# A hybrid decoder trunk on one core: weights issued ahead of cached pages, and evictions taken between the operations of the rotation

## The reference

```python
h = rmsnorm(x, norm_g);  proj = h @ w_in        # 1024 -> all mixers and gates
out_lru = (rg_lru(conv(lru_x)) * silu(lru_z)) @ w_lru_out
q, k = rope(rmsnorm(nsa_q)), rope(rmsnorm(nsa_k))
o_nsa = g0 * o_cmp + g1 * o_slc + g2 * o_win    # block means, top 16 blocks of 64, window of 512
out_nsa = (o_nsa * silu(nsa_z)) @ w_nsa_out     # keys and values: new rows and, for samples, cached pages
out_dn = (rmsnorm(gated_delta(conv(dn_qkv))) * silu(dn_z)) @ w_dn_out
merged = sigmoid(m0) * out_lru + sigmoid(m1) * out_nsa + sigmoid(m2) * out_dn
x = x + merged @ w_out
```

## Time and profile before

| what | value |
|---|---|
| median of 3 runs (lowest to highest) | 2092.81 us (2089.54 to 2092.93) |
| profiled execution, its own time | 2090.35 us |
| its span, first to last instruction | 2088.5 us |
| mean granted TensorE clock | 0.945 |
| busy, share of the span: PE, DVE, ACT, POOL | 88%, 45%, 25%, 4% |
| DMA, mean over the span | 81 GB/s |

### The profile page before, as it was taken

One profiled execution on the slowest core, in us unless ns is written; L12 is line 12 of the kernel. 1 busy time (PEld: TensorE's weight loads), 2 busy tenths in 40 slices (PEclk: granted clock), 3 DMA queues, 4 the chain that ended last, 5 costly groups with the idle time before them and its releaser, 6 DMA issues.

```text
span 2088.5 us, 29550 instructions
## 1 busy us (share of the span) xinstructions
PE 1842.8 (88%) x11486; PEld 1323.4 (63%) x11486; DVE 946.0 (45%) x2208; ACT 515.9 (25%) x1161; POOL 91.5 (4%) x133
## 2 busy tenths in 40 slices
PE   7999999998499955599999999999984998655999
PEld 5777787875355644477467767888652556444763
DVE  2558546336265432243135675453462653333421
ACT  3143211123266310110112341111322662110100
POOL 0001000011000000000000010100120000000000
PEclk9999999989799987899999999999997999887999
DMA  6214111123410233426042141111333103443321
GB/s 214 67 60 106 42 42 42 56 72 85 129 51 11 82 110 101 133 89 187 1 162 64 61 106 42 26 37 56 109 92 104 31 11 93 123 118 97 113 88 46
DMA packets 196528, 170.07 MB, mean 81 GB/s; under 512 B 49248, under 2 KB 186898, under 8 KB 195942
## 3 DMA queue, kind: packets, MB, share of 16 engines
q1 hardware_dynamic: 192164, 150.11, 24.7%
q0 software_dynamic: 4064, 18.03, 2.7%
q10 hardware_dynamic: 162, 0.05, 0.0%
HBM read 153.67 MB, written 21.71 MB: 84 GB/s over the span
## 4 chain that ended last, share of the span: by engine, by line
PE 75%; DVE 10%; SPq 7%; issue 4%; DMA 3%; ACT 1%; ACTq 0%; DVEq 0%
PE PS L920 49%; PE PS L849 5%; SPq L643 3%; DVE arena L1854 3%; DMA ring<-in_w_in 3%; SPq L655 3%; PE PS L1292 2%; PE PS L1305 2%; PE PS L1140 1%; PE PS L1122 1%; DVE arena L1780 1%; PE PS L1142 1%; PE PS L1361 1%; PE PS L1211 1%; PE PS L1026 1%
## 5 line engine op out<-in xcount | busy, mean ns | idle before, releaser
L920 PE MATMUL PS<-hT,ring 128*128 128x288 f32 x2624 | 692.3, 411 | 6.4 <-DVE arena L2057 3.7
L920 PEld LDWEIGHTS PS<-hT,ring 128*128 128x128 f32 x2624 | 488.4, 191 | 143.9 <-issue 11.7
L920 PE MATMUL PS<-zs,owr 128*128 128x288 f32 x768 | 215.6, 424 | 126.2 <-DVE sg L1786 126.2
L920 PEld LDWEIGHTS PS<-zs,owr 128*128 128x128 f32 x768 | 143.5, 197 | 170.5 <-DVE sg L1786 127.6
L920 PE MATMUL PS<-tt,ws 128*128 128x288 f32 x672 | 190.4, 415 | 11.8 <-DVE sg L1910 4.4
L849 PE MATMUL PS<-con,arena 128*128 128x128 f32 (+5 forms) x934 | 148.5, 286 | 13.4 <-DMA arena<-in_nsa_k_norm 10.7
L849 PEld LDWEIGHTS PS<-con,arena 128*128 128x128 f32 (+5 forms) x934 | 111.6, 144 | 74.2 <-issue 46.0
L920 PEld LDWEIGHTS PS<-tt,ws 128*128 128x128 f32 x672 | 120.7, 190 | 51.9 <-DVE sg L1910 8.0
L1786 DVE TENSOR_TENSOR ws<-ring 128x512 f32<-128x512 f32 x84 | 58.1, 691 | 201.8 <-DMA ring<-in_w_in 200.3
L920 PE MATMUL PS<-arena 128*128 128x512 f32 (+1 forms) x320 | 124.8, 594 | 2.1 <-DVE sg L1910 2.1
L1783 DVE TENSOR_TENSOR sg<-PS,sg 128x288 f32<-128x288 f32 x132 | 60.3, 457 | 134.6 <-PE PS L920 132.6
(11 more groups left out here) (303 smaller groups left out, 2060.9 us busy)
## 6 DMA issues: line engine op xcount, KB each, us to landing
ring<-in_w_in SPq DMA_DIRECT2D x54, 1024.0 KB, 5.4
arena<-in_cache_nsa_kv SPq DMA_DIRECT2D x128, 192.0 KB, 2.5
ring<-in_w_in SPq DMA_DIRECT2D x32, 256.0 KB, 4.3
arena<-in_state_nsa_win SPq DMA_DIRECT2D x32, 256.0 KB, 3.3
arena<-in_cache_nsa_kv SPq DMA_DIRECT2D x128, 64.0 KB, 1.8
arena<-in_w_out SPq DMA_DIRECT2D x4, 2048.0 KB, 8.1
out_win_sample<-in_state_nsa_win POOLq DMA_DIRECT2D x2, 4032.0 KB, 23.1
arena<-in_x_prompt SPq DMA_DIRECT2D x8, 512.0 KB, 5.3
```

Source lines behind the costliest of these rows:

```text
L920: ins = mm(to, w, x, start=start, stop=stop, skip_group_check=True)
```

## The change

On SyncE, `weights` and `out_weights` of the attention and sample stages are moved ahead of page loads: tile 22 ahead of the three waits and of the first key pages; `out_weights` 4 and 5 and tile 23 between the first key and value pages; tile 24 and `out_weights` 6 to 9 follow the first value pages. In the loop over pairs, `weights(25+k2)` becomes the first call of a step (it was behind both page batches), and the two `out_weights` come between the key pages and the wait for `s_pv`. The same DMAs are issued, with the same waits of their own.

On DVE, `take_to` is called at three places in the rotation of the key rows: after the product of `zs`, between the first two multiplies, and ahead of the addition.

```diff
@@ SyncE @@
                 out_weights(l * NO + 3)
+                weights(l * NS + 22)
                 sp.wait_ge(s["b_out"], l * 32 + 32)
                 sp.wait_ge(s["dn_ok"], past["dn_ok"] + 1)
                 sp.wait_ge(s["qk_ok"], past["qk_ok"] + 2)
                 cached_keys(0)
                 window_keys(0)
+                out_weights(l * NO + 4)
+                out_weights(l * NO + 5)
+                weights(l * NS + 23)
                 cached_values(0)
                 window_values(0)
-                for g in (22, 23, 24):
-                    weights(l * NS + g)
-                    for o in range(2):
-                        out_weights(l * NO + 2 * (g - 20) + o)
+                out_weights(l * NO + 6)
+                out_weights(l * NO + 7)
+                weights(l * NS + 24)
+                out_weights(l * NO + 8)
+                out_weights(l * NO + 9)
                 sp.wait_ge(s["a_p"], past["a_p"] + N_UNIT)
                 window_keys(1)
                 window_values(1)
                 for k2 in range(DEC_BATCH // 2):
+                    weights(l * NS + 25 + k2)
                     if k2 < DEC_BATCH // 2 - 1:
                         sp.wait_ge(s["s_t"], past["s_t"] + 6 * (k2 + 1))
                         cached_keys(k2 + 1)
                         for b in (2 * k2 + 2, 2 * k2 + 3):
                             window_keys(b)
+                    for o in range(2):
+                        out_weights(l * NO + 10 + 2 * k2 + o)
+                    if k2 < DEC_BATCH // 2 - 1:
                         sp.wait_ge(s["s_pv"], past["s_pv"] + k2 + 1)
                         cached_values(k2 + 1)
                         for b in (2 * k2 + 2, 2 * k2 + 3):
                             window_values(b)
-                    weights(l * NS + 25 + k2)
-                    for o in range(2):
-                        out_weights(l * NO + 10 + 2 * k2 + o)
@@ VectorE @@
                 mul(zs[:, 8:12], zs[:, 8:12], dc[:, 0:4]).then_inc(s["dn_ok"], 1)
+                normed = began[("bc_ok", past["bc_ok"] + 10)]
+                take_to(normed + 1)
...
                     link(mul(y, y, rep(C("sin"), m - n)))
                     if n == 0:
                         take_before("kt_t", 2)
+                    else:
+                        take_to(normed + 2)
                     link(mul(x, x, rep(C("cos"), m - n)))
                     if n == 0:
                         take_before("kt_t", 3)
+                    else:
+                        take_to(normed + 3)
                     add(x, x, y).then_inc(s["qk_ok"], 1)
```

## The result

| what | before | after |
|---|---|---|
| median of 4 runs (lowest to highest), us | 2092.87 (2089.54 to 2095.19) | 1887.76 (1882.57 to 1889.64) |
| profiled execution, its own time, us | 2090.35 | 1882.57 |
| its span, us | 2088.5 | 1880.8 |
| mean granted TensorE clock | 0.945 | 0.995 |

The ratio is 0.9017, 95% interval 0.8995 to 0.9039: faster by 205 us. The forecast was 1887 for the median and 1884.4 for the profiled execution. In the code after, the lines of TensorE, of ScalarE and of VectorE's helpers stand 6 higher (L920 is L926, L1786 is L1792), VectorE's lines behind the rotation 12 (L2251 is L2263); those of SyncE's loads are unchanged.

The account below looks back on a forecast made before the run. Weight tiles queued behind page loads on SyncE were taken to stall VectorE and then TensorE. 139.4 + 62.6 - 3.0 + 7.0 = 206.0 us off 2090.35 gave 1884.4, a median of 1887; range 1876 to 1912.

Parts of the forecast that it names:

- Pair loop: Three later sample pairs of each layer: with the weight tile issued first, halts and slow restarts go, worth 139.4 us.
- slow restart: TensorE after each halt: it runs on at the lower clock, costing 2.2 us each time.
- rival 1: Pair loop: SyncE's queue becomes the bound, 38.75 us a step against TensorE's 36.75; 12 us, giving 1899; chance 0.12.
- bound kept for late keys: Pair loop: last keys taking the weights' 5.4 us make the third batch 1.3 us late, 2.6 both layers; taken as 0.
- rule that the prediction weighed: Pair loop: key pages behind a 1 MB tile on one ring report after it; sum 2.6 us smaller, taken as 0.
- Attention: Attention stage, both layers: tile 22 issued earlier removes the halt and restart, 62.6 us, less 3 for late `out_weights` 4.
- 1.5 us taken off for `out_weights` 4 coming late: Attention, each layer: `out_weights` 4, now behind the first keys, is next late; bounds nothing or 4 us, -3 in all.
- Rotation: Key-row rotation on VectorE: evictions taken between its operations let TensorE's transposes start earlier; 3.5 us a layer, 7.0.
- Rival 2: Attention: the halt only moves, to `out_weights` 4 or tile 23; 59.6 us back, giving 1947; chance 0.05.
- Rivals 3 and 4: SyncE: 3, the tile leaves when it did, 2086 or 2093, chance 0.01; 4, pages late instead, 2132, chance 0.02.

## Why the prediction was right

**The size.** Profile to profile 207.7 us came, 3.4 of them in unchanged code; 204.3 is the change's, and the terms had 206.0.

**Pair loop, predicted 139.4, measured 136.6.** The reading that a tile is late by what stands before it on SyncE's queue held, and so did the slow restart after each halt: without halts the granted clock stays 1.00. Missing are 0.72 + 0.85 + 0.95 = 2.5 us of new waits, all in the last pair of a layer. That is rival 1 in small, and it comes from a step that was mis-sized: the margin was worked out with a step of 38.75 us, and the trace has 39.27 for the first and 40.07 for the second (750.13 to the next tile at 790.20). The row of one `weights` was taken at its 0.51 us, but SyncE's next page load begins 0.77 us later (710.86 + 0.51 to 712.14), and likewise 0.78 behind the output weights (730.03 + 1.06 to 731.87), which in turn took 1.06 us and not 1.6. The run with the windows on GpSimd, its step 1.6 us shorter, has none of these waits. The bound kept for late keys, 1.3 us a layer, was of the right size; late `owr` in this loop was in no term, though the prediction's own times have no margin for it: the last pair's two `out_weights` are issued from 805.8 to 807.4 and take 4.6 us or more, and TensorE wants them 2.5 us into the pair (774.64 - 0.72 - 771.38), at 811.2.

**The ring order.** Key pages directly behind the tile took 2.5 to 5.6 us to land (shortest and longest of 712 to 731), and 2.3 to 3.2 in the batch of 670 to 690, which isn't directly behind one; their medians are 3.2 and 2.4. In 712.14 to 729.01 the DMA engines were busy 0.81, where before it was 0.59. This agrees with the rule that the prediction weighed (the Trainium skill, "DMA: Bandwidth & Descriptors", Queues, rings and completion order): what stands behind a large transfer on a ring reports later. But it is the batch's first pages that pay (5.4 to 5.6 us for the first two, 2.6 to 3.0 for the last three), and TensorE waits for the last. The one late batch, 0.95 us in layer 1, isn't the ring's doing either: its last three pages landed in 2.4 to 3.0 us, and the wait is gone when SyncE's step is shorter while pages still follow the tile. So taking 0 for the rule was right. The tile itself took longer than assumed, 7.4 to 9.7 us in the pair loops against the 5.4 of the earlier trace rows; the 10 us that it was early covered it.

**Attention, predicted 59.6, measured 59.6, and that close by luck.** Three errors of one layer met. The first: the 1.5 us taken off for `out_weights` 4 coming late weren't lost. It went out at 530.20 and TensorE used it at 536.42 without a wait; its two DMAs landed in 4.1 to 4.3 us. From issue to use are 6.2 us, and 6.2 and 6.1 in the two runs with the old rotation, so the rotation's gain, which moves keys and use alike, isn't the reason. The prediction had 3.9 us there (538.6 to 542.5). It let `out_weights` 4 leave when the value pages used to, and counted its use as if the whole halt went.

That is the second error: the last 1.9 us of the halt stay. They are the work that the tile releases on VectorE, three weight sums, and behind them the reduction and ScalarE's eviction on which TensorE's next score waits. VectorE before and after, where the sums begin:

```profile
561.95 0.69 DVE L1786 TENSOR_TENSOR ws<-ring 128x512 f32<-128x512 f32 x1 [26.98 <-DMA ring<-in_w_in]
```

```profile
527.37 0.68 DVE L1792 TENSOR_TENSOR ws<-ring 128x512 f32<-128x512 f32 x1
```

Before, TensorE went on at 566.02, 4.07 us after the sums began; after, at 531.42, 4.05 us after. TensorE's own steps now cover 2.16 of it, and 1.89 stay open. VectorE has no pause from the sums to that reduction at 529.29; no run took the sums away. The third: the restart was worth 2.7 us and not 2.2. Between the first score and the first pooling of layer 0 TensorE was busy 135.45 us before and 132.76 after, with the same 711 passes. In sum 1.5 + 0.5 - 1.9 = 0.1 us a layer.

**Rotation, predicted 7.0, measured 4.1 + 4.1 in the trace,** 6.5 with its interval 4.0 to 8.8 from the takes alone. The gaps of 2.4 + 1.0 were 2.07 + 0.63, and the query rows begin 3.5 us earlier, once the 3.4 ahead are taken off, for the predicted 3.0. TensorE's first transposes come 4.1 earlier; the prediction worked out 3.7 and took 3.5.

**The rivals.** Rival 1 came with 2.5 us of its 12. Rival 2 (the halt only moves) didn't come in the whole change, but the run with the tile alone shows it for the pair loop: it is what happens when one of the two transfers is left behind the pages. I had costed the two as one edit; that they are worth 137 us together, and apart 41 and nothing that can be told, stood nowhere in the prediction. Rivals 3 and 4 are excluded by SyncE's timeline: the tile leaves at 710.86 and the key pages follow it at 712.14.

## What to carry to other kernels

A transfer is late by what stands before it on its in-order queue, waits included: compare the time at which it is issued with the time at which its slot came free, and move together *all* transfers that the same user needs, since one left behind keeps most of the stall. Before moving, lay the queue's whole step, gaps between different kinds of issue included, beside the consumer's period: here the new order has next to nothing to spare by the last pair, and 9 us more per batch cost a third of the gain. Not all of a halt goes with its cause: the work that the late transfer releases is in it too, so follow that chain on each engine, not only on the queue, and keep what TensorE has no work to cover.

## What the runs showed of the hardware

Of the 3.4 us that came ahead of the change 2.7 are in TensorE's 64 passes of 16 columns on layer 0's recurrence gates. The same instructions in the kernel before and after, then the windows over them (columns as in the earlier trace rows):

```profile
426.11 11.33 PE L1211 MATMUL PS<-arena 128*128 128x16 f32 x64
```

```profile
425.93 8.61 PE L1217 MATMUL PS<-arena 128*128 128x16 f32 x64
```

```profile
426.11:437.44 11.33, 11.33 (x66) 11.33 (x65) 2.35 (x4) 0.00 (x0) 0.00 (x0) 0.61 0.00 0
```

```profile
425.93:434.54 8.61, 8.61 (x66) 8.61 (x65) 2.35 (x4) 0.00 (x0) 0.00 (x0) 0.82 0.00 0
```

The granted clock tells the long ones from the short ones: its mean was 0.61 over the 11.33 us and 0.82 over the 8.61, though TensorE was busy all the time. Both begin at 1.00. Before, the clock fell to 0.50 (the lower of the two levels, 1.2 GHz) during the third and fourth us; after, during the fifth and sixth. In the ten profiled executions these passes took 8.35, 8.40, 8.61, 8.94, 9.17, 9.48, 10.50, 11.18, 11.25 and 11.33 us at 0.85, 0.84, 0.82, 0.79, 0.77, 0.74, 0.67, 0.62, 0.62 and 0.61. Time by clock is 6.9 to 7.1 in each, and so it is in layer 1. The low clock lasts into what follows: the four transposes behind (L849, L855) took 1.06 us before, at 0.50, and 0.60 after, at 1.00, which is most of the rest of the 3.4. When in the passes the clock falls has no relation to what was changed, and why then stays open.

The passes of the two layers together took 17.0 to 21.9 us. Executions of one kernel differ by as much and more (1882.57 to 1889.64, the fastest at a mean clock of 0.995 and the others at 0.991 or 0.992); that this comes from here is likely and not shown, as only one of them was profiled. It is a trap for any comparison of absolute times in two traces: differences have to be taken stage by stage.

The second DMA of a page with the same register costs some 0.5 us of SyncE's queue (1.61 - 1.10; it starts 0.52 behind the first), though the issue itself is shown with 0.33.
